# RWKV scan: in odd heads the transposed inverse, Z, G and the removals lie with the two chunks exchanged, and TensorE makes the transposed diagonal

## The reference

```python
def step(state, inp):
    r_t, w_t, k_t, v_t, kk_t, a_t = inp
    sk = jnp.einsum('bhvk,bhk->bhv', state, kk_t)
    state = state * w_t[:, :, None, :] - sk[..., None] * (kk_t * a_t)[:, :, None, :] + v_t[..., None] * k_t[:, :, None, :]
    return state, jnp.einsum('bhvk,bhk->bhv', state, r_t)
...
_, ys = lax.scan(step, s0, (tm(rh), tm(wh), tm(kh), tm(vh), tm(kk), tm(ah)))
```

## Time and profile before

| what | value |
|---|---|
| median of three runs | 3709.26 us |
| the profiled execution, its own time | 3713.88 us |
| its span in the trace | 3712.1 us |
| mean granted clock of TensorE | 0.97 of full |
| the scan of the RWKV layer in the span | about 3085 to 3460 us |

### The profile page before, as it was taken

One profiled execution on the slowest core, in us unless ns is written; L12 is line 12 of the kernel. 1 busy time (PEld: TensorE's weight loads), 2 busy tenths in 40 slices (PEclk: granted clock), 3 DMA queues, 4 the chain that ended last, 5 costly groups with the idle time before them and its releaser, 6 DMA issues. The chain is left out here.

```text
span 3712.1 us, 64726 instructions
## 1 busy us (share of the span) xinstructions
PE 3467.2 (93%) x27290; PEld 2028.3 (55%) x27290; DVE 1865.9 (50%) x2911; ACT 1154.8 (31%) x2214; POOL 864.9 (23%) x544
## 2 busy tenths in 40 slices
PE   8999999999998999899999999998899997887998
PEld 3447874445555777544455447444444335877543
DVE  3336652323218999631466228224658874665322
ACT  1127760102224555311311028112213352221124
POOL 0000003440000000242333210333126660333532
PEclk9999999999998999999999999999999998998999
DMA  6000013226235455510522020111264535443400
GB/s 244 29 23 2 2 45 127 88 71 173 77 102 143 126 134 133 196 46 17 181 81 80 0 91 2 68 46 18 89 235 174 201 135 155 118 113 82 165 12 40
DMA packets 312102, 358.43 MB, mean 97 GB/s; under 512 B 161540, under 2 KB 215028, under 8 KB 309126
## 3 DMA queue, kind: packets, MB, share of 16 engines
q1 hardware_dynamic: 311816, 354.30, 29.8%
HBM read 255.88 MB, written 98.29 MB: 95 GB/s over the span
## 5 line engine op out<-in xcount | busy, mean ns | idle before, releaser
L2200 DVE TENSOR_SCALAR_CACHE_REDUCE la_s<-psum 128x1280 f32<-128x1280 f32 x128 | 190.7, 1491 | 35.3 <-PE psum L2244 27.6
L2169 ACT ACTIVATE la_s<-la_s,la_negm 128x1280 f32<-128x1280 f32 x128 | 174.4, 1362 | 82.2 <-DVE la_s L2200 82.2
L970 POOL TENSOR_TENSOR lg_seven_s<-other_columns 128x512 f32<-128x512 f32 x4 | 5.1, 1264 | 732.3 <-POOLq L112 711.8
L991 PE MATMUL psum<-room,x_rows 128*128 128x512 f32 x320 | 145.6, 598 | 5.7 <-POOL x_rows L970 5.7
L970 POOL TENSOR_TENSOR wg_seven_s<-other_columns 128x512 f32<-128x512 f32 x5 | 6.3, 1268 | 592.3 <-POOLq L112 544.6
L835 DVE CUSTOM_DVE_ANT_0 wa_s<-psum,window_mask_rows 128x640 f32<-128x640 f32 (+1 forms) x128 | 100.6, 786 | 71.6 <-PE psum L890 71.6
L3328 POOL TENSOR_TENSOR x_rows<-x_rows,pg_g 128x512 f32<-128x512 f32 x56 | 84.0, 1500 | 153.7 <-DVE pg_g L3477 140.2
L991 PE MATMUL psum<-room,rp_seven_s 128*128 128x512 f32 x256 | 115.2, 593 | 3.2 <-DVE rp_seven_p L1040 3.2
L793 ACT ACTIVATE wa_s<-wa_s,wa_negm 128x640 f32<-128x640 f32 (+2 forms) x160 | 117.3, 742 | 0.4 <-DVE wa_negm L838 0.3
L991 PE MATMUL psum<-rp_t,rp_seven_s 128*128 128x512 f32 x256 | 117.0, 600 | 0.0
L991 PEld LDWEIGHTS psum<-room,x_rows 128*128 128x128 f32 x320 | 60.5, 192 | 77.8 <-issue 77.8
(11 more groups left out here) (719 smaller groups left out, 7947.4 us busy)
## 6 DMA issues: line engine op xcount, KB each, us to landing
x_rows<-rwkv_raw SPq DMA_DIRECT2D x40, 512.0 KB, 4.8
room<-rwkv_raw SPq DMA_DIRECT2D x33, 512.0 KB, 5.2
later_slot<-in_ada_w_dram SPq DMA_DIRECT2D x16, 1024.0 KB
rwkv_raw<-x_rows SPq DMA_DIRECT2D x64, 256.0 KB, 2.9
rwkv_raw<-x_rows SPq DMA_DIRECT2D x32, 512.0 KB, 4.2
room<-in_odd_w_in_dram SPq DMA_DIRECT2D x6, 2048.0 KB, 13.0
first_weights<-latent_v SPq DMA_DIRECT2D x32, 320.0 KB, 5.4
la_v<-latent_v SPq DMA_DIRECT2D x32, 320.0 KB, 5.5
```

Of the source, the lines that this page charges most:

```text
L991: last = pe.matmul(bank, left[:, k, :], right[:, k, :], start=fresh and k == 0, stop=k == HK - 1, skip_group_check=True)
L2169: act.activation(s, s, ACT.Exp, scale=-1.0, bias=negm[:, u % RING:u % RING + 1], accum_out=total[:, head(u) % 2, tile(u):tile(u) + 1]).the ...
L2200: dve.tensor_scalar(by_lane(s_sb[:, u % RING, :]), by_lane(banks_of(scores_side(u)))[:, :, 0:SPAN], -SCALE, FAR, ALU.mult, ALU.min, accum_ ...
```

## The change

- Where the product of head h and chunk c has a choice of side, `side(h, c)` is now half c for even heads and half 1-c for odd heads. Z, TT, G and the removal rows e0 of odd heads lie with the two chunks exchanged; A, T (plane 0), U, the values and the state stay as they were.
- The removal rows are therefore loaded by three DMAs (`sp_removals`): the even heads, and the odd heads of each chunk into the other half.
- `quad` reads its moving operand for odd heads so that the removal columns come from the other chunk.
- z writes into two banks (2 and 3, or 0 and 1), join into two (4 and 5, or 6 and 7), even and odd heads apart. VectorE's join is two instructions of 256 columns in the first level.
- Only the plain 16 x 16 inverses are no longer sent: `small_t` alone is written and placed on plane 0, and the placed half of `diagonal` alone is zeroed. Plane 1 is made by `turn_diagonal`: 32 products with the identity into banks 6 and 7, ahead of z(0), and ScalarE copies them in two halves (`move_diagonal`).

```diff
+    REMOVAL_LOADS = 3
+    def sp_removals(self, sp, i, to):
+        by_pair = lambda t: t.rearrange("p (n e d) -> p n e d", e=2, d=W_DIM)
+        chunk = lambda c: slice(c * W_CHUNK, (c + 1) * W_CHUNK)
+        source = self.raw[4][self.at(i), :]
+        sp.dma_start(by_pair(to)[:, :, 0, :], by_pair(source)[:, :, 0, :]).then_inc(self.e0_in[i % 2], 16)
+        for c in range(2):
+            sp.dma_start(by_pair(to[chunk(1 - c), :])[:, :, 1, :], by_pair(source[chunk(c), :])[:, :, 1, :]).then_inc(self.e0_in[i % 2], 16)
...
+        side = lambda h, c: chunk(c if h % 2 == 0 else 1 - c)
+        z_banks, join_banks = (lambda m: core.banks(2 - 2 * (m % 2), 2)), (lambda m: core.banks(4 + 2 * (m % 2), 2))
+        turned_banks = core.banks(6, 2)
...
                 def load_removals(i):
-                    sp.dma_start(e0[i % 2], raw[4][at(i), :]).then_inc(e0_in[i % 2], 16)
+                    scan.sp_removals(sp, i, e0[i % 2])
...
-                    sp.dma_start(scan.inverses.rearrange("u q s -> q u s"), small_both).then_inc(q["small_out"], 16)
+                    sp.dma_start(scan.inverses, small_t).then_inc(q["small_out"], 16)
...
-                        sp.dma_start(diagonal[g * B:(g + 1) * B, :, :, t].rearrange("p u h t -> p (u h) t"), inverses[g]).then_inc(q["diagonal_in"], 16)
+                        sp.dma_start(diagonal[g * B:(g + 1) * B, 0, :, t], inverses[g]).then_inc(q["diagonal_in"], 16)
...
-                pool.memset(diagonal[:, :, :, :], 0.0).then_inc(q["zeroed"], 1)
+                pool.memset(diagonal[:, 0, :, :], 0.0).then_inc(q["zeroed"], 1)
...
                 def move_started(i):
                     act.wait_ge(q["g_prod"], i + 1)
-                    copy(G[:, :, :], core.banks(0, 2).rearrange("p (h d) -> p h d", h=H)).then_inc(q["g_moved"], 1)
+                    copy(pairs(G[:, :, :]), apart(core.banks(0, 2))).then_inc(q["g_moved"], 1)
...
+                def move_diagonal(i):
+                    act.wait_ge(q["diagonal_turned"], i + 1)
+                    if i:
+                        act.wait_ge(q["joined"], (i - 1) * UNITS + GROUPS)
+                    for half in range(2):
+                        some = slice(half * PAIRS // 2, (half + 1) * PAIRS // 2)
+                        copy(pairs(diagonal[:, 1, :, :])[:, some, :, :], apart(turned_banks)[:, some, :, :]).then_inc(q["diagonal_moved"], 1)
...
                         move_output(i - 1)
                     move_started(i)
+                    move_diagonal(i)
...
-                    act.activation(U[:, :, :], core.banks(4, 2).rearrange("p (h d) -> p h d", h=H), ACT.Copy, scale=-1.0).then_inc(q["tg_moved"], 1)
+                    act.activation(pairs(U[:, :, :]), apart(core.banks(4, 2)), ACT.Copy, scale=-1.0).then_inc(q["tg_moved"], 1)
...
                 def move_z(i, m):
                     dve.wait_ge(q["z_made"], i * UNITS + (m + 1))
-                    tt(grp(Z, m), core.banks(2 + m % 2)[:, 0:GH * C].rearrange("p (h t) -> p h t", h=GH),
-                       for_heads(levels[:, m // GROUPS, :], GH), ALU.mult).then_inc(q["z_moved"], 1)
+                    tt(parted(grp(Z, m)), first_columns(z_banks(m)), levels[:, m // GROUPS, :].unsqueeze(1).unsqueeze(1).broadcast_to([P, 2, GH // 2, C]),
+                       ALU.mult).then_inc(q["z_moved"], 1)
...
                 def join(i, m):
                     dve.wait_ge(q["join_made"], i * UNITS + (m + 1))
-                    first = 0 if m < UNITS - GROUPS else 1
-                    part = inv[:, first:, (m % GROUPS) * GH:(m % GROUPS + 1) * GH, :].rearrange("p u h t -> p u (h t)")
                     held = diagonal if m < GROUPS else inv
-                    old = held[:, first:, (m % GROUPS) * GH:(m % GROUPS + 1) * GH, :].rearrange("p u h t -> p u (h t)")
-                    tt(part, old, core.banks(4 + m % 4).rearrange("p (u c) -> p u c", u=2)[:, first:, :], ALU.add).then_inc(q["joined"], 1)
+                    if m < UNITS - GROUPS:
+                        tt(parted(grp(T, m)), parted(grp(held[:, 0, :, :], m)), first_columns(join_banks(m)), ALU.add)
+                    tt(grp(TT, m), grp(held[:, 1, :, :], m), join_banks(m)[:, GH // 2 * C:(GH // 2 + GH) * C].rearrange("p (h t) -> p h t", h=GH), ALU.add).then_inc(q["joined"], 1)
...
+                within_group = lambda n: slice((n % 2) * BANK + (n // 2) * C, (n % 2) * BANK + (n // 2 + 1) * C)
...
-                                last = pe.matmul(out, src[rows, p, chunk(c)], xT[rows, i % 2, p, :, chunk(c)], start=True, stop=True)
+                                right = xT[rows, i % 2, p, :, chunk(c)]
+                                if e:
+                                    four = xT[rows, i % 2, p, :, :].rearrange("p u (s t) -> p (u s) t", t=C)
+                                    right = four[:, 0:4:3, :] if c else four[:, 1:3, :]
+                                last = pe.matmul(out, src[rows, p, chunk(c)], right, start=True, stop=True)
...
-                            last = pe.matmul(core.banks(0, 2)[chunk(c), head(h)], A[chunk(c), i % 2, h, 1, :], v[i % 2][chunk(c), head(h)], start=True, stop=True)
+                            last = pe.matmul(core.banks(0, 2)[side(h, c), split(h)], A[chunk(c), i % 2, h, 1, :], v[i % 2][chunk(c), head(h)], start=True, stop=True)
...
+                    if m == 1:
+                        pe.wait_ge(q["g_moved"], i + 1)
...
-                            last = pe.matmul(core.banks(2 + m % 2)[chunk(c), n * C:(n + 1) * C], A[chunk(c), i % 2, h, 0, :], before[chunk(c), 0, h, :],
+                            last = pe.matmul(z_banks(m)[side(h, c), within_group(n)], A[chunk(c), i % 2, h, 0, :], before[chunk(c), 0, h, :],
...
                 def join(i, m):
-                    if m >= 4:
-                        pe.wait_ge(q["joined"], i * UNITS + (m - 3))
+                    if m >= 2:
+                        pe.wait_ge(q["joined"], i * UNITS + (m - 1))
                     elif m == 0:
                         pe.wait_ge(q["a_masked"], min(i + 2, NT) * QUADS * 2)
-                    elif m == 2 and i:
-                        pe.wait_ge(q["y_moved"], i)
+                    if m % 2 == 0 and m < GROUPS:
+                        pe.wait_ge(q["diagonal_moved"], 2 * i + m // 2 + 1)
+                    if m == 1:
+                        pe.wait_ge(q["diagonal_moved"], 2 * i + 2)
                     pe.wait_ge(q["z_moved"], i * UNITS + (m + 1))
-                    bank = core.banks(4 + m % 4)
+                    banks = join_banks(m)
                     before = (diagonal if m < GROUPS else inv)[:, 1, :, :]
-                    for n in range(GH):
-                        h = (m % GROUPS) * GH + n
+                    for first in range(0, GH, 2):
+                        both = [(n, (m % GROUPS) * GH + n, c) for n in range(first, first + 2) for c in range(CHUNKS)]
                         if m < UNITS - GROUPS:
-                            for c in range(CHUNKS):
-                                pe.matmul(bank[chunk(c), n * C:(n + 1) * C], before[chunk(c), h, :], Z[chunk(c), h, :], start=True, stop=True)
-                        for c in range(CHUNKS):
-                            last = pe.matmul(bank[chunk(c), (GH + n) * C:(GH + n + 1) * C], Z[chunk(c), h, :], before[chunk(c), h, :],
+                            for n, h, c in both:
+                                pe.matmul(banks[chunk(c), within_group(n)], before[side(h, c), h, :], Z[side(h, c), h, :], start=True, stop=True)
+                        for n, h, c in both:
+                            last = pe.matmul(banks[side(h, c), (GH // 2 + n) * C:(GH // 2 + n + 1) * C], Z[side(h, c), h, :], before[side(h, c), h, :],
                                              start=True, stop=True)
                     last.then_inc(q["join_made"], 1)
+                def turn_diagonal(i):
+                    pe.wait_ge(q["diagonal_in"], (i + 1) * PLACES * 16)
+                    pe.wait_ge(q["a_masked"], min(i + 2, NT) * QUADS * 2)
+                    if i:
+                        pe.wait_ge(q["y_moved"], i)
+                    for h in range(H):
+                        for c in range(CHUNKS):
+                            last = pe.matmul(turned_banks[side(h, c), split(h)], diagonal[chunk(c), 0, h, :], core.ident[chunk(c), chunk(c)], start=True, stop=True)
+                    last.then_inc(q["diagonal_turned"], 1)
...
                 def inverse(i):
+                    turn_diagonal(i)
                     z(i, 0)
...
-                            last = pe.matmul(core.banks(2 + c)[at(h), (h // 2) * C:(h // 2 + 1) * C], e0[i % 2][chunk(c), head(h)], TT[chunk(c), h, :],
+                            last = pe.matmul(core.banks(2 + c)[at(h), (h // 2) * C:(h // 2 + 1) * C], e0[i % 2][side(h, c), head(h)], TT[side(h, c), h, :],
...
-                            last = pe.matmul(core.banks(4, 2)[chunk(c), head(h)], TT[chunk(c), h, :], G[chunk(c), h, :], start=True, stop=True)
```

(11 more changed lines are left out.)

6 lines of the change are left out of this document (3 added, 3 removed).

## The result

The changed kernel takes 3717.48 us (median of 17 runs, 3712.08 to 3722.52), the one before 3709.12 beside it: ratio 1.0015, interval 1.0008 to 1.0022. (The two medians alone are 8.4 us, 0.23%, apart.) It is slower, by about the 0.2% that the prediction called measurable, where 16 us less were forecast. The profiled execution has

A forecast was written before the change was run, and what follows sets the result against it. The scan's serial chain was taken as the bound, the inverse being TensorE's with VectorE close behind. Terms -1.3 + 0.9 - 1.3 - 0.4 = -2.1 us a tile, -16 over eight: 3693 us from the median; range 3682 to 3708.

The forecast's parts named there:

- part 1: Ahead of z(0): placing one plane instead of two by DMA saves 1.3 us a tile, bounds nothing and -2.5.
- Part 2: Head of the inverse: making the transposed diagonal on TensorE and ScalarE costs 0.9 us a tile, bounds +0.4 and +1.4.
- Part 3: Rest of the inverse: shorter units, VectorE becoming the first level's bound, save 1.3 us a tile, bounds -0.6 and -1.6.
- part 4: weigh_started in four quarters saves 0.8 us, but from_state waits for HmT's copy, so 0.4 a tile; bounds 0 and -0.5.
- added instruction fetches: Whole scan: with tile 0's missing output_sums, only "a little less" gain, taking the sum from -16.8 to -16 us.
- Rival (a): Placing: nine DMAs set its time, not their pieces, so no gain there; 3703 us; chance 0.17 with a neighbouring case.
- The four quarters: TensorE's small products: using all four quarters of the array halves their cost, 15 ns a record instead of 27.
- (c): TensorE's small products: a floor of 25 ns a record shrinks the gains to -1.3 us a tile, 3699 us; chance 0.03.
- (e): TensorE's products: quarters do not overlap when even and odd heads alternate; 3713 us; chance 0.03.
- the mean's side: Inverse: of a saving between 0.8 and 1.4 us a tile, 1.3 was taken, against the mean of 13.7 over eight tiles.
- Rival (b): Inverse and weighings: TensorE, less busy, stays at the low clock, +1.2 us a tile, 3719 us; chance 0.07.

The follow-up runs named there:

- exchange_only: The changed kernel with both planes placed by DMA as before and no turn of the diagonal; ratio 1.0000 to the kernel before.
- no_turn: The changed kernel without turn_diagonal and ScalarE's copies of it, one plane placed and plane 1 left zeros; ratio 0.9970 to the kernel before.
- after_no_bulk: The changed kernel with the loads of queries and keys of tiles 3 to 7 cut to 16 x 16 elements; ratio 0.9978 to the kernel before.

## Why the prediction was wrong, point by point

**The sum, in its own terms.** By the ratios, the placing (part 1) gave 11 us where 10.4 were forecast; the turn cost 17; the exchange gave 0, and 15 with the bulk loads cut. Part 2's 8 x 0.9 = 7.2 was the turn less the exchange's faster head, which is 0.5 us a tile (below). With that put to the exchange, about 11 were forecast for the turn and, with parts 3 and 4, 17.6 for the exchange. So the step that failed most is that "added instruction fetches" were put at next to nothing; the turn's price was mis-sized by a third.

**Part 1, the placing, was right in kind; its size is uncertain.** Forecast -10.4 us; 7.0 in the stretches, of which 3.1 are in exchange_only too, whose placing is as before; 5.2 in the stretches and 0.30% (11 us) by the ratios between exchange_only and no_turn, 0.16% with the loads cut. Rival (a), that it gives nothing, falls. The issue went from 486 to 448 ns and the landing from 2.4 to 2.2 us at the median, the DMA out to the first placing issue from 2.9 to 1.8:

```profile
3338.03 0.32 SPq L4514 DMA_DIRECT2D rwkv_inverses<-room  x1
3339.79 4.69 SPq L4522 DMA_DIRECT2D first_weights<-rwkv_inverses  x8
```

```profile
L4522 SPq DMA_DIRECT2D first_weights<-rwkv_inverses x64: 318/448/1669, 3119.1 to 3427.5; - x64
...
DMA to landing us min/median/max: 2.0/2.2/3.6
```

**The four quarters are worth what was said.** After the change weigh_removals and weigh_started start 0.98 us apart, and the next product 1.33 later, behind the HmT copy (after_no_bulk, tile 2):

```profile
3219.79 1.16 PE L4953 MATMUL psum<-rs_inverse,room 64*64 64x64 f32 x64 [1.25 <-DVE rs_inverse L4766]
3220.77 1.11 PE L4961 MATMUL psum<-rs_G,rs_inverse 64*64 64x64 f32 x64
3222.10 0.27 PE L4969 MATMUL psum<-rs_S,rs_HmT 64*64 64x64 f32 x2 [0.21 <-ACT rs_HmT L4620]
```

From weigh_removals to from_state are 2.31 us instead of 2.73, so part 4 is -0.42, forecast -0.4. In tiles 2 to 6 the changed kernel's third stretches are 2.6 us shorter in all (five tiles); tiles 0 and 1, with stops of 1.3 to 1.6 us in them, are 5.6 longer. Rivals (c) and (e) fall.

**Part 2: the head came out, the turn costs more.** VectorE's first join was forecast 4.4 us after the first product. The rows of tiles 4 and 7:

```profile
3306.26 0.42 DVE L4762 TENSOR_TENSOR rs_inverse<-first_weights,psum 128x256 f32<-128x256 f32 x1 [0.28 <-PE psum L4924]
...
3433.89 0.42 DVE L4762 TENSOR_TENSOR rs_inverse<-first_weights,psum 128x256 f32<-128x256 f32 x1 [0.81 <-PE psum L4924]
```

It is at 4.14 in tile 7, at the low clock, and that is the forecast's mechanism, 0.6 over the 3.5 of the kernel before. The 4.54 of tile 4 agrees by luck: there the clock is full, and TensorE stops for 1.90 us inside z(0). The exchange alone moves this join to 3.0 (exchange_only, tile 7, also at the low clock), so what the turn adds in the head is 1.1 us a tile, while by the ratios it costs 2.1 a tile in all. The other 1.0 is not in the head; TensorE's "issue" idle time is 30 us with the turn and 20 without (no_turn), 18 and 14 with the loads cut, and part of it could lie there. Joined in one term with the exchange's faster head, the turn's price was hidden. A change without the turn is what would have paid.

**Part 3 failed first by its base.** The chain was worked out as 8.8 us from VectorE's first join; undisturbed it is 9.0 (exchange_only, tile 7: 3422.48 to 3431.50). The whole inverse was forecast as 13.2 us and is 13.26 in tile 7, where nothing disturbs it (the 13.19 of tile 1, at the full clock and with a stop of 1.23 us in it, agrees by luck). But 13.2 was set against a mean of 13.7, "the mean's side", and the kernel before takes 13.17 undisturbed as well: what stands above that in its mean (109.9 - 8 x 13.2 = 4.3 us) is for 3.3 us TensorE's "issue" idle time, which the change could not save. The gain of parts 2 and 3 together was 0 from the start, not -3.2 us.

**The step that decided is the one costed at nothing: the instruction fetches.** "Added instruction fetches" were put into "a little less" by their count, and the count is small: 222 packets for 218. What matters is when a packet has to pass. In the changed kernel the disturbance of the inverses is 118.1 - 8 x 13.3 = 11.7 us instead of 4.3, and the third stretch and the last tile have 6.3 us more where part 4 said 3.2 less. The loads, kept in full, take 0.40 points (about 15 us, good to 8) of the exchange's gain, and the cut shows it. 1.4 us of the last tile is the port collision above, met there by chance (0.69 us became 2.13):

```profile
3455.37 1.90 POOL L4584 TENSOR_TENSOR x_rows<-room,rs_bonus 128x1024 f32<-128x1024 f32 x1 [3.88 <-DMA rwkv_y<-x_rows]
```

```profile
3455.69 2.13 DVE L4780 TENSOR_TENSOR rs_S<-rs_S,rs_eC 128x512 f32<-128x512 f32 x1
```

**Rival (b)** had the sign and nearly the time (3719), by another way. Its main argument does not hold here, that a low clock makes the inverse longer than before: exchange_only runs an inverse at a mean clock of 0.75 in 12.26 us, faster than the kernel before at 0.87; VectorE sets the pace there. The low clock costs where it follows a stall into work that TensorE bounds. (The 0.98 that the prediction held against this rival, as of stretches behind the inverse, is of tile 5's stretch ahead of it.)

**Open.** Why the exchange makes the packets late more often is not settled. The number of matmuls is the same as before (exchange_only has 27290, as before), the packets are as many, and the order of products differs. So does the load of the removals: three DMAs in 256-byte pieces in every kernel with the exchange, and no run has the exchange without them. That denser bursts of products use up instructions sooner, so that the next packet falls into the loads, is only argued. Where in the program the packets are asked for was not varied. Nor is it shown that a packet waits for the loads in front of it: the long stops fit that, but at 3371.2 us a packet started and passed while the engines were fully busy with loads.

## What to carry to other kernels

Take the base of a saving from an undisturbed tile, and name what stands above it in the mean: a shorter chain does not remove another stream's waits. Before a stretch of small matmuls is made denser, look at the instruction queue's packets beside the bulk loads on SP, and try those loads spread. And when a reduction on VectorE is moved, see what GpSimd starts by it, and beside which VectorE product of two SBUF operands that will lie.

## What was not expected of the hardware

Beside bulk loads (two of 512 KB; the last time weights of 2 MB), a 16 KB instruction packet came late: in the changed kernel's four longest stops (ending at 3271, 3316, 3360 and 3450 us, 2.4 to 3.3 us each) it started 6.5 to 7.5 us after the packet before it, where the median is 4.7, behind 2 us in which the DMA engines were nearly all busy, and TensorE went on 2.2 to 2.4 us after its start. These stops were followed by 6.8 us or more at 1.2 GHz. GpSimd's 2.36 us operation stretched a VectorE product of two SBUF operands from 0.69 to 1.99 us, at most 2.83, and left the same shape with a PSUM operand alone.
